# The opening of a two-block decoder kernel: gates from unsplit x, splits ahead of squares

## What is computed

```
def rmsnorm(x, g):
    xf = x.astype(jnp.float32)
    y = xf * lax.rsqrt(jnp.mean(xf * xf, axis=-1, keepdims=True) + EPS)
    return (y * g.astype(jnp.float32)).astype(x.dtype)
...
    proj = xn @ w_in
    qkv = jax.nn.silu(causal_dwconv(proj[..., :A_CONV_WIDTH], conv_w))
    ...
    b_raw = proj[..., A_CONV_WIDTH + A_V_WIDTH:A_CONV_WIDTH + A_V_WIDTH + A_HEADS]
    a_raw = proj[..., A_CONV_WIDTH + A_V_WIDTH + A_HEADS:]
    q = _l2norm(...) * (A_HEAD_K ** -0.5)
    k = _l2norm(...)
    beta = jax.nn.sigmoid(b_raw.astype(f32))
    g = -jnp.exp(A_log.astype(f32)) * jax.nn.softplus(a_raw.astype(f32) + dt_bias.astype(f32))
    o = chunk_gated_delta_rule(q, k, v, beta, g).astype(xn.dtype)
```

## Time and profile before

| | us |
|---|---|
| median of 3 runs | 1764.39 |
| lowest, highest | 1764.36, 1766.49 |
| the profiled execution's own time | 1764.32 |
| its span, first to last instruction | 1762.7 |
| TensorE busy in the span | 1742.7 (99%) |
| VectorE busy | 1124.5 (64%) |
| ScalarE busy | 860.2 (49%) |
| GpSimd busy | 40.0 (2%) |

### The profile page before, as it was taken

The page is one execution under the profiler, slowest core; times in us unless marked ns, Lnnn a source line. Parts: engine busy times, 40 slices in busy tenths (PEclk is TensorE's granted clock), DMA queues, the critical chain, the costliest instruction groups (busy, mean ns, idle before and its releaser), DMA issues.

```text
span 1762.7 us, 25377 instructions
## 1 busy us (share of the span) xinstructions
PE 1742.7 (99%) x9070; PEld 1363.7 (77%) x9070; DVE 1124.5 (64%) x1842; ACT 860.2 (49%) x1359; POOL 40.0 (2%) x71
## 2 busy tenths in 40 slices
PE   9999999999999999999999999999999999999998
PEld 6777777778888888788887788888887766777886
DVE  7788888567777733567776677777433555765444
ACT  6656566444444432467776444444333466643222
POOL 2000000000000000000000000000000000100000
PEclk9999999999999999999999999999999999999999
DMA  5522221133332322243331332323321312323321
GB/s 186 186 75 70 73 73 48 49 120 95 95 95 95 107 98 82 84 116 112 102 102 61 118 89 92 95 95 107 106 85 52 108 36 73 102 72 108 95 95 60
DMA packets 45832, 163.51 MB, mean 93 GB/s; under 512 B 5841, under 2 KB 8164, under 8 KB 45760
## 3 DMA queue, kind: packets, MB, share of 16 engines
q1 hardware_dynamic: 40864, 148.00, 26.1%
q0 software_dynamic: 4464, 14.47, 2.8%
q10 hardware_dynamic: 432, 0.07, 0.0%
HBM read 155.89 MB, written 6.63 MB: 92 GB/s over the span
## 4 chain that ended last, share of the span: by engine, by line
PE 91%; issue 3%; DVE 3%; ACT 2%; DMA 1%; POOL 0%; SPq 0%; DVEq 0%; ACTq 0%; POOLq 0%
PE acc L609 23%; PE acc L610 23%; PE acc L611 23%; PE acc L635 8%; PE pa L609 1%; PE pa L610 1%; PE pa L611 1%; PE pbc L994 1%; PE pbc L1069 1%; ACT wsplit L1210 1%; PE pa L1057 1%; PE pa L738 1%; PE pd L1007 1%; PE pd L1082 1%; PE pd L1006 1%
## 5 line engine op out<-in xcount | busy, mean ns | idle before, releaser
L1210 ACT ACTIVATE wsplit<-wraw 128x1024 fp32r<-128x1024 f32 (+1 forms) x250 | 274.1, 1098 | 439.6 <-PE acc L611 400.8
L609 PE MATMUL acc<-xhi,wsplit 128*128 128x512 f32 x1200 | 487.5, 406 | 1.1 <-DVE at_vs L2215 1.0
L611 PE MATMUL acc<-xhi,wsplit 128*128 128x512 f32 x1200 | 475.6, 396 | 0.0
L610 PE MATMUL acc<-xlo,wsplit 128*128 128x512 f32 x1200 | 475.5, 396 | 0.0
L1767 DVE TENSOR_TENSOR wsplit<-wraw,wsplit 128x1024 fp32r<-128x1024 f32 (+1 forms) x247 | 314.4, 1274 | 141.8 <-ACT wsplit L1210 140.9
L609 PEld LDWEIGHTS acc<-xhi,wsplit 128*128 128x128 f32 x1200 | 225.9, 188 | 68.5 <-issue 14.0
L611 PEld LDWEIGHTS acc<-xhi,wsplit 128*128 128x128 f32 x1200 | 225.9, 188 | 54.7
L610 PEld LDWEIGHTS acc<-xlo,wsplit 128*128 128x128 f32 x1200 | 226.4, 189 | 51.4 <-issue 1.4
L635 PE MATMUL acc<-xhi,wsplit 128*128 128x512 f32 x464 | 158.2, 413 | 0.1
L610 PE MATMUL acc<-hid_lo,wsplit 128*128 128x512 f32 x352 | 139.6, 396 | 0.0
L611 PE MATMUL acc<-hid_hi,wsplit 128*128 128x512 f32 x352 | 139.6, 396 | 0.0
(11 more groups left out here) (417 smaller groups left out, 2484.2 us busy)
## 6 DMA issues: line engine op xcount, KB each, us to landing
wraw<-w SPq DMA_DIRECT2D x220, 512.0 KB, 3.6
wraw<-w SPq DMA_DIRECT2D x32, 704.0 KB, 4.1
bias_dram<-ext_dram POOLq DMA_DIRECT2D x1, 4096.0 KB, 23.2
bias<-bias_dram POOLq DMA_DIRECT2D x16, 256.0 KB, 3.0
at_ks<-at_ks SPq DMA_DIRECT2D x16, 256.0 KB, 2.9
crow<-row_dram POOLq DMA_DIRECT2D x8, 256.0 KB, 3.7
brow<-row_dram POOLq DMA_DIRECT2D x8, 256.0 KB, 4.5
h<-xT SPq DMA_DIRECT2D x3, 512.0 KB, 7.8
```

Of the source, the lines that this page charges most:

```text
L609: mm(out, whi[:, k, :], a[:, x_at + k, :], start=(k == first), stop=False)
L610: mm(out, whi[:, k, :], b[:, x_at + k, :], start=False, stop=False)
L611: m = mm(out, wlo[:, k, :], a[:, x_at + k, :], start=False, stop=(k == last))
L1210: A(split(s, i, j, 0), raw(s, j), ACT.Copy).then_inc(w_hi_ready, 1)
```

## The change

In words:

- The gates are computed from x as it landed, in full precision, with x as the stationary operand: for each k, four matmuls (128 tokens each) against 16 columns, `wg_gain`, the gate weights times the norm's gain, made by one small VectorE operation. They come out with tokens in partitions, so the transposes, the padded and split gate weights and two memsets go. They need the sum of squares for each token in that layout too: four more small matmuls, and its root, `rtok`, on ScalarE.
- TensorE: 4 waking matmuls instead of 7, two before k=0, one before k=1, one before k=2. Gates k=0 to 5, then tile 1 for k=0 to 3, gates 6 and 7, tile 1 for k=4 to 7, sums by token, the norm's sum, tile 2.
- ScalarE and VectorE: all splits of x come before the squares of k=2 to 7, which ScalarE makes in pairs; the tokens' root and the first gate step come ahead of the norm's root; the second `conv_newest` comes ahead of the table load for `silu`, and the square of k ahead of that of q.
- VectorE: the block mask moves from behind the take of tile 3 to ahead of the gates; the low half of tile 3's weight moves from ahead of the gates to behind two taps.
- GpSimd no longer waits for the gates before two memsets.

The diff, cut to its core:

```diff
-WAKING = 7
+WAKING = [2, 1, 1, 0, 0, 0, 0, 0]
...
-        wg_hi = r.sb("wg_hi", [P, KD, P], F32R)
-        wg_lo = r.sb("wg_lo", [P, KD, P], F32R)
+        wg_gain = r.sb("wg_gain", [P, KD, 16])
+        gates = r.sb("gates", [P, NC, 16])
+        rtok = r.sb("rtok", [P, NC, 16])
...
             nc.gpsimd.memset(rr[:], 0.0).then_inc(ev("zeroed"), 1)
-            nc.gpsimd.memset(wg_hi[:].bitcast(F32), 0.0).then_inc(ev("zeroed"), 1)
-            nc.gpsimd.memset(wg_lo[:].bitcast(F32), 0.0).then_inc(ev("zeroed"), 1)
             nc.gpsimd.memset(xm[:], 0.0).then_inc(ev("zeroed"), 1)
             pool.dma_start(relf[:], rel_flip).then_inc(ev("tables_landed"), 16)
             nc.gpsimd.memset(negs[:], NEG).then_inc(ev("zeroed"), 1)
-            pool.wait_ge(ev("gate_pe"), at(GATE_PE, "gates_done"))
             nc.gpsimd.memset(tn[:], 0.0).then_inc(ev("zeroed"), 1)
             nc.gpsimd.memset(tt[:], 0.0).then_inc(ev("zeroed"), 1)
...
-            for n in range(WAKING):
-                mm(pd[:], rr[:, 0, :], rr[:].rearrange("p t q -> p (t q)"), start=True, stop=True)
+
+            def gates_of(k):
+
+                for n in range(WAKING[k]):
+                    mm(pd[:], rr[:, 0, :], rr[:].rearrange("p t q -> p (t q)"), start=True, stop=True)
+                if k in X_PARTS:
+                    pe.wait_ge(ev(f"x_landed{X_PARTS.index(k)}"), 16)
+                if k == 0:
+                    pe.wait_ge(ev("wg_scaled"), 1)
+                for t in range(NC):
+                    mm(pb[:, t * 16:t * 16 + 16], h[:, k, t * P:t * P + P], wg_gain[:, k, :], start=(k == 0 and t == 0), stop=(k == KD - 1 and t == NC - 1))
+
+            def early_tile(s, j, k0, k1):
+                for k in range(k0, k1):
+                    pe.wait_ge(ev("x_lo_ready"), k + 1)
+                    tile(s, -1, j, k0=k, k1=k + 1)
+
             s = st["delta"]
-            for k in range(KD + 3):
-                if k < KD:
-                    pe.wait_ge(ev("x_lo_ready"), k + 1)
-                    if k == 0:
-                        pe.wait_ge(ev("wg_lo_ready"), 1)
-                    mm(acc[:, 2, :], wg_hi[:, k, :], xhi[:, k, :], start=(k == 0), stop=False)
-                    mm(acc[:, 2, :], wg_hi[:, k, :], xlo[:, k, :], start=False, stop=False)
-                    m = mm(acc[:, 2, :], wg_lo[:, k, :], xhi[:, k, :], start=False, stop=(k == KD - 1))
-                    if k == KD - 1:
-                        m.then_inc(ev("gate_pe"), 1)
-                if k >= 3:
-                    tile(s, -1, 1, k0=k - 3, k1=k - 2)
+            for k in range(6):
+                gates_of(k)
+            early_tile(s, 1, 0, 4)
+            gates_of(6)
+            gates_of(7)
+            early_tile(s, 1, 4, KD)
             pe.wait_ge(ev("consts_landed"), 32)
+            pe.wait_ge(ev("ssq_added"), KD)
+            for t in range(NC):
+                m = mm(pb[:, 64 + t * 16:64 + t * 16 + 16], ssq[:, t * P:t * P + P], cst[:, C_ONE, 0:16], start=True, stop=True)
+            m.then_inc(ev("gate_pe"), 1)
             norm(0)
-            tile(s, -1, 2, k1=3)
-            pe.wait_ge(ev("gate_dve"), at(GATE_DVE, "gates_copied"))
-            for t in range(NC):
-                m = turn(pb[:, t * 16:(t + 1) * 16], sq[0:16, 0, t * P:t * P + P], cst[0:16, C_ID, 0:16])
-            m.then_inc(ev("gate_pe"), 1)
-            tile(s, -1, 2, k0=3, k1=6)
+            tile(s, -1, 2, k1=6)
...
             for k in range(KD):
                 if k in X_PARTS:
                     act.wait_ge(ev(f"x_landed{X_PARTS.index(k)}"), 16)
                 split_x(0, gains(G_A), xhi, k)
-                if k >= 4:
-                    act.wait_ge(ev("ssq_added"), k - 3)
-                A(normed(k), h[:, k, :], ACT.Square).then_inc(ev("h_squared"), 1)
-                if k == 0:
-                    act.wait_ge(ev("wg_landed"), 16)
-                    act.wait_ge(ev("zeroed"), 2)
-                    A(wg_hi[:, :, 0:16], wg[:], ACT.Copy).then_inc(ev("wg_hi_ready"), 1)
-                if k == 2:
+                if k < 2:
+                    squares(k, k + 1)
+                if k == 3:
                     cast(s, -1, 1)
+            squares(2, 4)
+            act.wait_ge(ev("ssq_added"), 2)
+            squares(4, 6)
+            act.wait_ge(ev("ssq_added"), 4)
+            squares(6, 8)
             cast(s, -1, 2)
             act.wait_ge(acc_done, 1)
             cast(s, -1, 3)
-            root(0)
-
-
+            act.wait_ge(ev("gate_pe"), at(GATE_PE, "tokens_summed"))
+            A(rtok[:].rearrange("p t c -> p (t c)"), pb[:, 64:128], ACT.Ln, bias=eps_d, scale=1.0 / D).then_inc(ev("gate_act"), 1)
+            act.wait_ge(ev("gate_act"), at(GATE_ACT, "tokens_ln"))
+            A(rtok[:], rtok[:], ACT.Exp, scale=-0.5).then_inc(ev("gate_act"), 1)
             act.wait_ge(ev("gates_landed"), 32)
             A(alog[:], alog[:], ACT.Exp).then_inc(ev("gate_act"), 1)
+            gate_cols = gates[:].rearrange("p t c -> p c t")
+            act.wait_ge(ev("gate_dve"), at(GATE_DVE, "gates_ready"))
+            A(t0[:], gate_cols[:, 0:8, :], ACT.Exp, scale=-1.0).then_inc(ev("gate_act"), 1)
+            root(0)
+            act.wait_ge(ev("gate_dve"), at(GATE_DVE, "gate_abs"))
+            A(t1[:], t1[:], ACT.Exp, scale=-1.0).then_inc(ev("gate_act"), 1)
+            act.wait_ge(ev("gate_act"), at(GATE_ACT, "gate_exp"))
+            A(t1[:], t1[:], ACT.Ln, bias=1.0).then_inc(ev("gate_act"), 1)
...
-            act.wait_ge(ev("gate_pe"), at(GATE_PE, "gates_turned"))
-            gates = pb[:, 0:64].rearrange("p (t c) -> p c t", c=16)
-            A(t0[:], gates[:, 0:8, :], ACT.Exp, scale=-1.0).then_inc(ev("gate_act"), 1)
             act.wait_ge(ev("consts_landed"), 32)
             conv_newest(1, 0, -1)
-            act.wait_ge(ev("gate_dve"), at(GATE_DVE, "gate_abs"))
-            A(t1[:], t1[:], ACT.Exp, scale=-1.0).then_inc(ev("gate_act"), 1)
-            act.wait_ge(ev("gate_act"), at(GATE_ACT, "gate_exp"))
-            A(t1[:], t1[:], ACT.Ln, bias=1.0).then_inc(ev("gate_act"), 1)
             act.wait_ge(ev("gate_dve"), at(GATE_DVE, "kes_diff"))
             A(ecl[:].rearrange("p h t -> p (h t)"), pb[:, 32:64], ACT.Exp).then_inc(ev("gate_act"), 1)
             A(nbe[:], cc[:], ACT.Exp).then_inc(ev("gate_act"), 1)
             A(kes[:], kes[:], ACT.Exp).then_inc(ev("gate_act"), 1)
+            conv_newest(2, 0, -1)
             tables("silu_and_others")
             silu(-1, 1)
-            conv_newest(2, 0, -1)
             cast(s, 0, 0)
             silu(-1, 2)
+            square_k(-1)
             square_q(0)
-            square_k(-1)
             tables("natural_log_exp_and_others")
...
-            for k in range(KD):
-                split_x(0, gains(G_A), xhi, xlo, k)
-                if k == 0:
-                    dve.wait_ge(ev("wg_hi_ready"), 1)
-                    dve.wait_ge(ev("zeroed"), 3)
-                    tt_(wg_lo[:, :, 0:16], wg[:], wg_hi[:, :, 0:16].bitcast(F32), ALU.subtract).then_inc(ev("wg_lo_ready"), 1)
+            dve.wait_ge(ev("wg_landed"), 16)
+            tt_(wg_gain[:], wg[:], gains(G_A).to_broadcast([P, KD, 16]), ALU.mult).then_inc(ev("wg_scaled"), 1)
+
+            def add_square(k):
                 dve.wait_ge(ev("h_squared"), k + 1)
                 if k > 0:
                     dve.wait_ge(ev("ssq_added"), k)
                 tt_(ssq[:], ssq[:], normed(k), ALU.add).then_inc(ev("ssq_added"), 1)
-                if k == 2:
+
+            for k in range(KD):
+                split_x(0, gains(G_A), xhi, xlo, k)
+                if k < 2:
+                    add_square(k)
+                if k == 3:
                     low(s, -1, 1)
+            for k in range(2, KD):
+                add_square(k)
             low(s, -1, 2)
-            low(s, -1, 3)
...
-            dve.wait_ge(ev("rstd_ready"), 1)
-            dve.wait_ge(ev("gate_pe"), at(GATE_PE, "gates_done"))
-            tt_(sq[0:16, 0, :], acc[0:16, 2, :], rstd[0:16, :], ALU.mult).then_inc(ev("gate_dve"), 1)
-            take(-1, 1)
-
-            gates = pb[:, 0:64].rearrange("p (t c) -> p c t", c=16)
+            dve.wait_ge(ev("consts_landed"), 32)
+            block8 = cst[:, C_BLOCK, :]
+            tt_(block8, cst[:, C_LOW, :], cst[:, C_LOW + 1, :], ALU.add).then_inc(ev("solve_dve"), 1)
...
+            dve.wait_ge(ev("gate_act"), at(GATE_ACT, "tokens_ready"))
+            tt_(gates[:].rearrange("p t c -> p (t c)"), pb[:, 0:64], rtok[:].rearrange("p t c -> p (t c)"), ALU.mult).then_inc(ev("gate_dve"), 1)
+            dve.wait_ge(ev("gate_dve"), at(GATE_DVE, "gates_ready"))
+
+            gate_cols = gates[:].rearrange("p t c -> p c t")
             hc = [P, HA, NC]
+            dve.wait_ge(ev("gates_landed"), 32)
+            tt_(gg[:], gate_cols[:, 8:16, :], dtb[:].unsqueeze(2).to_broadcast(hc), ALU.add).then_inc(ev("gate_dve"), 1)
+            dve.wait_ge(ev("gate_dve"), at(GATE_DVE, "gate_sum"))
```

(9 more changed lines are left out.)

42 lines of the change are left out of this document (20 added, 22 removed).

## The result

| | before | changed |
|---|---|---|
| median of 20 runs, us | 1764.47 | 1768.4 |
| lowest | 1763.9 | 1764.75 |
| highest | 1766.49 | 1775.55 (one more, at 5999.84, is left out) |
| profiled execution, its span | 1764.32, 1762.7 | 1767.75, 1766.1 |

The changed kernel's median counts all 20 runs; without the one at 5999.84 us it is 1767.75. The ratio of the times is 1.0021, with a 95% interval of 1.0014 to 1.0028: the changed kernel is slower by 0.2%, and its times are spread over 11 us where those of before lie within 3.

A forecast was written before the change was run, and what follows sets the result against it. TensorE was taken to bound the kernel, its chain lying there for 91%. Gains of 0.85 + 0.3 + 0.3 = 1.45 us off 1764.32 gave 1762.9 us; own range 1761.9 to 1763.9, wider range 1761.0 to 1766.3.

The forecast's parts named there:

- the opening's clock: TensorE before tile 2: lower level through gates k=0, upper level afterwards; tile 2 at 22.25 against 22.74, 0.5 us gained.
- The rival's mechanism: TensorE's opening: narrow 16-column gate matmuls delay the clock's rise or lower it; chances 0.18 mild, 0.07 grave.
- The grave form: Clock rival in the opening: lower level until tile 1 has run for 5 us, about 8 us lost, 1771; chance 0.07.
- The mild form: Clock rival in the opening: rise one step later or one spell at the lower level, some 1.7 us, 1764.6; chance 0.18.
- The row that argued against them: Against the clock rival: no stretch of the trace shows a fall, the solves' 32-column matmuls included.
- Price of the new products: Gates' and token sums' 36 matmuls on TensorE: 0.22 us each, 0.11 a record; bounds 0.11 and 0.30.
- Four loads for each matmul: Rival at the 36 new matmuls: four loads of 0.11 us each, 7.9 us more, near 1771 us; chance 0.03.
- The turned gates: The gates' four transposes on TensorE and their wait on VectorE all go: 0.76 us gained.
- the new wait: TensorE ahead of the cumulative sums' turns waits for VectorE's later copy: 0.3 to 0.4 us, 0.4 given back.
- The squares of k: TensorE's wait before k's squares are summed: the 0.3 us stays, start at about 35.15, lead 0.85 us.
- V's turn: TensorE's 0.32 us wait before v is turned goes, silu of v coming 1.1 us earlier: 0.3 us gained.
- The rows of head 1: Rows queued behind the bias table on POOL land near 71 instead of just before 75.36 us: 0.3 us gained.

The follow-up runs named there:

- e3: Changed kernel with the bias table's copy held back behind head 1's rows and head 0's solved blocks; median 1765.06 us, ratio 1.0010.
- e1: The changed kernel run again without any edit, for a second trace; median 1769.97 us, ratio 1.0020 to the kernel before.
- e9: Kernel before plus 24 full-precision 16-column matmuls, results thrown away, between its seven waking matmuls and its gates; 1772.13 us, ratio 1.0036.
- e5: Changed kernel with its four waking matmuls in one piece ahead of the gates of k=0; median 1767.51 us, ratio 1.0014 to the kernel before.
- e15: Kernel before with six more wide waking matmuls (13 instead of 7); 1768.21 us, ratio 1.0020.
- e6: Changed kernel with six waking matmuls in one piece ahead of the gates; median 1766.30 us, ratio 1.0009 to the kernel before.
- e2: Changed kernel with one more waking matmul before the gates of k=3 and one before k=4; median 1773.13 us, ratio 1.0031 to the kernel before.
- e16: Changed kernel with 512-column gate products, wakings two and one, bias table's copy where the changed kernel has it; median 1762.38 us, ratio 0.9989 to before.
- e10: Kernel before with only the 4 MB bias table copy moved behind head 1's rows and the first system; 1764.09 us, ratio 0.9997.
- e4: Changed kernel with wakings added before k=3 and k=4 and the bias table's copy held back; median 1771.21 us, ratio 1.0021 to the kernel before.
- e14: Changed kernel with 512-column gate products over 16 stationary weight columns, wakings two and one, bias table's copy late; median 1762.35 us, ratio 0.9986 to before.
- e13: Changed kernel with 512-column gate products, wakings two, one and one, bias table's copy late; median 1762.94 us, ratio 0.9990 to the kernel before.
- e17: Changed kernel with 512-column gate products, only the two wakings at the start, bias table's copy late; median 1762.27 us, ratio 0.9988 to before.

## Why the prediction was wrong

**The step that failed is the opening's clock**: "Gates k=0 at the lower level, 8 records of 0.21 us: 6.85", and from there on everything at the upper level. It has two parts, rise and fall, and both fail. The waking piece of two matmuls made the rise a matter of chance: 12 of 30 executions lie in the group that the profiles of e3 and e1 show, low to 23 us. And where it rose, six k's of gates in a row let it fall. The profiled execution, by the working's own steps, against the forecast second pass of tile 2 at 22.25 + 0.23 = 22.48 us: the gates of k=4 start at 11.84 instead of 11.2, since x landed later (+0.64); they take 3.43 to the start of tile 1 instead of 1.75 (+1.68); the twelve passes take 4.27 instead of 2.8 (+1.47); the rest 6.57 instead of 6.73 (-0.16). That is 22.48 + 3.63 = 26.11.

**The rival's mechanism was right, its chance was not.** The grave form was told as "the lower level lasts until tile 1 has run for 5 us", 1771; e1's and e3's profiles show just that, and the group lies at 1769.0 to 1770.6. The mild form, 1764.6, is the group at 1764.7 to 1765.7. They had 0.07 and 0.18, and hold 22 of 30 executions. The row that argued against them was read wrongly: the narrow matmuls elsewhere in the trace stand among wide passes, as the prediction itself said, and e9 shows what they do when they stand alone. The row that spoke for them, the rise only after 5 us of wide work, was given too little weight: the change cut that piece from seven matmuls to two. The sum also took one course for all executions, where the median of a mixture can lie at neither. The range ended at 1766.3 and thus left out the group at 1770.

The Trainium skill, TensorE: Matmul & The Clock Gate, Part 1, says that what decides is not tied to the kernel's start, so that the same kernel rises at different points from run to run. This case agrees, by the spread of the rise in one kernel from 5 to 23 us. Of the kernel before, whose wide work is dense from 1.46 us on, 141 of 162 executions took less than 1765.5 us, 1 us above the median.

**Price of the new products: right.** 16 records at the upper level, from 19.54 us, are followed by the next instruction at 21.24, so 1.70 us, 0.11 a record. Four loads for each matmul are excluded.

**The turned gates and the new wait.** The transposes went, 0.76. The wait ahead of the turns is 0.1 us, not 0.4: the last pass starts at 31.70, 0.23 later the turns could start, and they do at 32.05, as VectorE's copy ends (31.82 and 0.18). With 0.1 less between the cumulative sums this stretch gained 0.75 where 0.36 was forecast.

**The squares of k: right.** The wait of 0.30 stayed.

**V's turn: right in size, wrong in the row.** The stretch is 0.39 us shorter (0.3 forecast), but the wait still reads 0.3; what shrank is VectorE's way from the sum of k's squares to the decay (42.69 - 35.98 = 6.71 us before, 44.69 - 38.37 = 6.32 now), where the wait of 0.31 us ahead of the decay went. GpSimd's last copy had ended at 42.60 us there, just before the decay's 42.69, so this wait went for the reason that was forecast. But silu of v came only 0.4 us earlier, counted from the sum of k's squares (46.32 - 35.98 against 48.33 - 38.37), not 1.1, and the wait ahead of v's turn did not go. GpSimd's copies start at 37.27 against 38.09 in an execution 3.1 us later, so 4 us earlier in its own time, as forecast.

**The rows of head 1: right.** The waits for `rr` went from 1.4 to 1.1 us.

**Not foreseen: the wait without releaser.** The earlier trace rows don't show it, but the kernel before had one of 0.41 us at 61.90. In the two profiles of the changed kernel and in e5's it is 2.0 to 2.5 us. It stands, in both kernels, after TensorE's record 345 or 346, counted in the trace. e15, the kernel before with twelve more waking records, has one of 0.85 us, again after record 345, so it goes by the number of records and not by the place in the program. In these five profiles the wait ends 2.2 to 2.5 us after the start of a packet of the instruction queue (59.7 us before, 61.8 changed, 65.5 e1, 63.4 e5, 63.8 e15); where that packet comes earlier (e6 by 58, e16 by 60 us, e2 6 us ahead of record 346) there is no wait. Queue, packets, MB, share of 16 engines, the changed kernel in 60 to 62 us and e16 in 56 to 60 us:

```profile
q8 instruction: 1, 0.02, 3.0%
```

```profile
q8 instruction: 1, 0.02, 1.5%
```

I read it as a block of instructions that is fetched too late. That fits all five profiles, but nothing was changed to test it, and neither the block's border nor the part of the 4 MB copy is shown: e10's profile, with the late copy, has the packet at 59.2 us and no wait, and e2, e6 and e16 have no wait with the early one. The Trainium skill, Runtime: NRT & Kernel Launch, section Instruction fetch mechanics, calls the crossing of such a border "mostly hidden"; if the wait is such a crossing, it took 2.25 us in the profiled execution. It has no part in the groups: executions of one course have the same time with the copy early and late. Left out of the changed kernel's profile, it takes that span to 1763.9, which with the 1.65 between span and time gives 1765.5, in the middle group.

**The whole.** The lowest execution of the changed kernel, 1763.2 us, lies in the group that e4's profile shows with a clock that stands; the forecast for that course was 1762.9. That nearness is in part luck. Behind the second pass the profiled execution gained 0.75 and 0.39 us, and 0.86 behind the solve with its wait of 2.25 us left out, 2.0 in all where 0.95 was forecast. By this estimate the opening of the execution at 1763.2, 1.3 us under the median of before, was not 0.5 us shorter than before but 0.7 longer. Behind the second pass of tile 2, e14 is 1739.73 - 1737.33 = 2.40 us shorter than the kernel before, where 1.45 - 0.5 = 0.95 was forecast for the change. By stretch that is 0.89 us to the sum of k's squares where 0.36 was forecast, 0.37 to v's turn for 0.3, and 1.14 behind the solve for 0.3. Of this last, 0.41 is the wait without releaser, which e14 has not, 0.31 the rows of head 1, and 0.4 have no row.

## What to carry to other kernels

Ask of every edit near the start what TensorE's clock sees of it: here the rise was sure when six or seven wide matmuls woke TensorE in one piece, or when two did and wide work followed almost at once, and the clock stayed in all 44 executions with wide gates. When a product can be laid either way, the one that streams many columns was the safer here at equal time, even with transposes behind it. And look at the spread of the times, not at one profile: where executions of one kernel fall into groups, a single profile shows one course of several.

## What the runs showed of the hardware

- A 16-column full-precision matmul under 128x128 weights occupies TensorE for 0.22 us at the upper level and yet the clock fell during stretches of them (e6 and e9 without any wait; the changed kernel beside waits of 0.6 us). In stretches of 512-column ones with only 16 stationary columns it did not (e13, e14, e16, e17).
- Narrow matmuls that follow a clock that is up don't always bring it down (one of five executions of e9 by its time, the group at 1763), and with two more wide ones between them (e2, e4) it stayed up in 8 of 12 executions that had it up, against 2 of 22 without.
- The clock fell beside idles too: within 0.3 us of the end of waits of 1.98 us (e1) and 2.53 us (e5), and 1.5 us behind one of 1.83 us in wide work (e10). It did not behind waits of 2.25 us (the changed kernel at 64 us) or 1.04 us (e17). No experiment varied an idle alone.
- The granted clock on the page and by stretch reads 1.00 at the start even where rows stand 0.43 us apart, until a first change is recorded (e1: "1.00" in every stretch, with rows at half speed until 23.4 us). The distance of equal rows is the surer sign.
- A wait without releaser, 0.4 to 2.5 us, stood after record 345 or 346 of TensorE in five profiles, and ended 2.2 to 2.5 us after the start of a packet of the instruction queue.
